# Gate and up tiles of a feed-forward layer as seven Strassen block products in place of eight

## The reference, cut to what matters

```python
def hybrid_layer(h, pos, states, p):
    u = rms_norm(h, p['norm_mix']) @ p['w_in']
    ...  # four groups of heads: SSD, retention, GLA, RG-LRU
    h = h + mixed.astype(h.dtype)          # mixed = concat(four outputs) @ w_out
    hn = rms_norm(h, p['norm_ffn'])
    h = h + ((jax.nn.silu(hn @ p['w_gate']) * (hn @ p['w_up'])) @ p['w_down']).astype(h.dtype)
```

## Time and profile before

| | us |
|---|---|
| median of 3 runs | 1392.7 |
| lowest, highest | 1392.46, 1395.43 |
| span of the profiled execution | 1392.0 |
| TensorE busy in it | 1361.7 |
| VectorE busy | 630.7 |
| ScalarE busy | 492.6 |
| GpSimd busy | 409.9 |

### The profile page before, as it was taken

One profiled execution on the slowest core, in us unless ns is written; L12 is line 12 of the kernel. 1 busy time (PEld: TensorE's weight loads), 2 busy tenths in 40 slices (PEclk: granted clock), 3 DMA queues, 4 the chain that ended last, 5 costly groups with the idle time before them and its releaser, 6 DMA issues.

```text
span 1392.0 us, 26025 instructions
## 1 busy us (share of the span) xinstructions
PE 1361.7 (98%) x11309; PEld 1313.6 (94%) x11309; DVE 630.7 (45%) x1250; ACT 492.6 (35%) x675; POOL 409.9 (29%) x204
## 2 busy tenths in 40 slices
PE   7999999999999999999999999999999999999996
PEld 7888898999999999999998888899999999999996
DVE  6844765553321343133757456646443123322434
ACT  6526454432221222122553364543322122222221
POOL 1101001434433443344400100023334433443341
PEclk9999999999999999999999999999999999999998
DMA  7746633222222223222466465422222222222231
GB/s 248 182 106 154 160 80 104 89 88 81 88 91 92 83 85 91 91 87 81 130 139 156 119 156 130 106 79 90 78 91 80 89 92 92 82 86 92 91 92 65
DMA packets 42066, 146.68 MB, mean 105 GB/s; under 512 B 5216, under 2 KB 6496, under 8 KB 41952
## 3 DMA queue, kind: packets, MB, share of 16 engines
q1 hardware_dynamic: 30672, 111.95, 25.1%
q0 software_dynamic: 6624, 24.12, 10.4%
q10 hardware_dynamic: 4656, 8.95, 2.1%
HBM read 137.34 MB, written 5.43 MB: 103 GB/s over the span
## 4 chain that ended last, share of the span: by engine, by line
PE 85%; DVE 7%; ACT 3%; DVEq 2%; issue 1%; ACTq 1%; DMA 0%
PE bank L1261 78%; DVE ct L755 1%; PE bank L1209 1%; DVE lru_x L755 1%; PE bank L1518 1%; ACT wl L419 0%; PE bank L1524 0%; PE bank L1225 0%; DVEq L754 0%; PE bank L1220 0%; ACT wh L420 0%; DVE h L1200 0%; PE bank L1443 0%; DVE gl_gla L1186 0%; PE bank L1547 0%
## 5 line engine op out<-in xcount | busy, mean ns | idle before, releaser
L1261 PE MATMUL bank<-xh,wh 128*128 128x272 f32 x2208 | 649.8, 294 | 7.9 <-DVE xl L710 7.6
L1261 PE MATMUL bank<-xh,wl 128*128 128x272 f32 x2208 | 642.9, 291 | 0.0
L1261 PE MATMUL bank<-xl,wh 128*128 128x272 f32 x2208 | 639.3, 290 | 0.0
L391 POOL TENSOR_TENSOR wl<-raw,wh 128x1024 fp32r<-128x1024 f32 x154 | 369.7, 2400 | 591.0 <-ACT wh L420 572.1
L1261 PEld LDWEIGHTS bank<-xh,wh 128*128 128x128 f32 x2208 | 420.0, 190 | 19.4 <-issue 17.5
L420 ACT ACTIVATE wh<-raw 128x1024 fp32r<-128x1024 f32 x199 | 210.2, 1056 | 611.3 <-PE bank L1261 611.3
L1261 PEld LDWEIGHTS bank<-xl,wh 128*128 128x128 f32 x2208 | 420.5, 190 | 1.0 <-issue 1.0
L1261 PEld LDWEIGHTS bank<-xh,wl 128*128 128x128 f32 x2208 | 419.3, 190 | 0.0
L1178 DVE TENSOR_TENSOR tz<-bank,rs_bcast 128x272 f32<-128x272 f32 x176 | 77.6, 442 | 293.3 <-PE bank L1261 289.3
L1158 DVE TENSOR_TENSOR h<-h,bank 128x272 f32<-128x272 f32 x128 | 55.4, 436 | 217.3 <-PE bank L1261 217.2
L397 POOL DMA_DIRECT2D wl<-weights x46 | 40.0, 870 | 365.2 <-ACT wl L419 365.2
(11 more groups left out here) (360 smaller groups left out, 1721.1 us busy)
## 6 DMA issues: line engine op xcount, KB each, us to landing
raw<-weights SPq DMA_DIRECT2D x202, 512.0 KB, 3.6
wl<-weights POOLq DMA_DIRECT2D x46, 512.0 KB, 6.9
h<-x SPq DMA_DIRECT2D x4, 544.0 KB, 6.0
y<-h SPq DMA_DIRECT2D x4, 544.0 KB, 2.7
rv<-rk ACTq DMA_DIRECT2D x8, 136.0 KB, 4.0
tz<-rq ACTq DMA_DIRECT2D x8, 136.0 KB, 5.4
S<-s_ssd ACTq DMA_DIRECT2D x2, 512.0 KB, 7.0
n_ssd<-Vx ACTq DMA_DIRECT2D x2, 512.0 KB, 2.8
```

What stands on the lines that cost most here:

```text
L391: nc.gpsimd.tensor_tensor(wl[:, s, :], raw[:, s, :], wh[:, s, :].bitcast(F32), ALU.subtract).then_inc(lo_done, 1)
L1261: ins = mm(bank_, wt[:, n % RING, w], xx[:, cols], start=(i == 0 and j == 0), stop=(i == len(ks) - 1 and j == 2))
```

## The change

The product of one pair is seen as blocks of 2 x 2: the 8 k-tiles are split in even (e) and odd (o) ones, the tokens in `first` and `second` half, and the two outputs are gate and up. Plain, that is eight block products of 4 k-tiles x 272 tokens x 3 passes. The Winograd form of Strassen's scheme takes seven:

- P1 and P2 are plain (gate even x first, gate odd x first), P3 and P4 have a sum on one side, P5 to P7 on both. Gate first = P1 + P2, and the others are sums of P1, P6, P7 and P3, P4 or P5. On the weight side P5, P7, P6 and P4 need sums of blocks of the gate and up units, on the side of the activations P5, P7, P3 and P6.
- **Weight sums.** VectorE makes them for every pair in `wsum`: `weight_sums` (1024 columns), `second_sum` and `last_sum` (512 each). The remainders of P6 and P5 are made by VectorE (`sum_low`), those of P4 and P7 by GpSimd, those of P1, P2 and P3 by accumulating transfers of 512 columns. ScalarE rounds all seven blocks, and negates three.
- **Sums of the activations.** Once per layer, while the output units run: `next_part`, `sums_hi` on ScalarE, `part_low`, `x_sums`, `x_sums_low` on VectorE.
- **Taking the results.** ScalarE copies P1 (`take_p1`), P1 + P6 (`take_u2`) and P1 + P6 + P7 (`take_u3`) out of a bank on which TensorE then goes on adding. VectorE adds and scales: `gate_first`, `gate_second`, `up_second`, `product`, `product_low`. P4 and P3 of a pair are computed during the next pair.
- **The ring.** `raw` has four slots. `wh` and `wl` are rings of eight half units of 512 columns (`RING`, `NEXT`): a product takes one, a plain unit two. ScalarE prepares the block that takes the place of a product as soon as that product is done (`hi_after`).
- **Output units.** Their remainders come by accumulating transfers now, as those of the input units.
- **Banks of the norm.** The statistics in front of the feed-forward part use `dense` banks (`norm_banks`). TensorE's order there is P1, P2, P6 and P5 of pair 0, most of it ahead of the last tile, then the spread of the factors, then P7.

```diff
+RING = 8
+WIDE = [2 if kind == "unit" else 1 for _, kind, _ in STEPS]
...
 def low_by(j):
...
+    return {"P1": FROM_HBM, "P2": FROM_HBM, "P3": FROM_HBM, "P4": ON_POOL, "P5": ON_VECTOR, "P6": ON_VECTOR,
+            "P7": ON_POOL}[kind]
...
 @block.sync
+                    sp.wait_ge(hi_done, step(layer, "P3" if u > gate_unit(p) else "P2", p) + 1)
+                    sp.wait_ge(sum_made.sem, sum_made.at(layer, 3 * p + 3))
...
 @block.scalar
+            def hi_block(j):
+                layer, kind, i = STEPS[j]
+                if kind in SUM_PLACE:
+                    act.wait_ge(sum_made.sem, sum_made.at(layer, 3 * i + SUM_MADE[kind]))
+                    whole = sum_cols(kind)
...
+                if LOW_BY[j] == FROM_HBM:
+                    a(wl[:, place(j)], whole, ACT.Copy, scale=-1.0).then_inc(negated, 1)
+                a(wh[:, place(j)], whole, ACT.Copy).then_inc(hi_done, 1)
...
+                for g, (p0, n) in enumerate(GROUPS):
+                    for p in range(p0, p0 + n):
+                        if p:
+                            take_p1(p)
+                        hi_after(step(layer, "P1", p))
+                        hi_after(step(layer, "P2", p))
+                        if p > p0:
+                            hi_after(step(layer, "P4", p - 1))
+                        take_u2(p)
+                        hi_after(step(layer, "P6", p))
+                        if p > p0:
+                            silu(p - 1)
+                            hi_after(step(layer, "P3", p - 1))
+                        hi_after(step(layer, "P5", p))
+                        take_u3(p)
+                        if p > p0:
+                            act_high(p - 1)
+                        hi_after(step(layer, "P7", p))
...
 @block.vector
+                def weight_sums(p):
...
+                    tt(wsum[:, 0:2 * BLOCK], raw_cols(n + 1), raw_cols(n, BLOCK), ALU.subtract).then_inc(sum_made.sem, 1)
...
+                def sum_low(kind, p):
+                    j = step(layer, kind, p)
+                    dve.wait_ge(hi_done, j + 1)
+                    tt(wl[:, place(j)], sum_cols(kind), wh[:, place(j)].bitcast(F32), ALU.subtract).then_inc(lo_vector, 1)
...
+                    for p in range(p0, p0 + n):
+                        more = p + 1 < p0 + n
+                        if more:
+                            weight_sums(p + 1)
+                        gate_first(p)
+                        if more:
+                            second_sum(p + 1)
+                        if more:
+                            last_sum(p + 1)
+                        if p > p0:
+                            gate_second(p - 1)
+                        if more:
+                            sum_low("P6", p + 1)
+                        if p > p0:
+                            product(p - 1)
+                        if more:
+                            sum_low("P5", p + 1)
+                        if p > p0:
+                            product_low(p - 1)
+                        up_second(p)
...
 @block.tensor
+                    for k in steps:
...
+                        for pass_, (wt, xx) in enumerate(((wh, hi), (wh, lo), (wl, hi))):
+                            ins = mm(b[:, 0:HALF], wt[:, at:at + P], xx,
...
+                product("P5", 0, rest, True)
+                spread_rstd(layer, 0)
+                product_7(0)
...
+                def product_7(p):
+                    pe.wait_ge(u2_taken.sem, u2_taken.at(layer, p + 1))
+                    product("P7", p)
...
+                        first_products(p)
+                        if p > p0:
+                            product_4(p - 1)
+                        product_6(p)
+                        if p > p0:
+                            product_3(p - 1)
+                        product_5(p)
+                        product_7(p)
```

More of the change, by code:

```diff
@@ L254, in trunk @@
         dense, M = bank[0:3], bank[3:8]
+        bank_a, bank_b, bank_c = M[0:2], M[2:4], M[4]
+        first, second = slice(0, HALF), slice(HALF, TOK)
         def cst(name, parts=P, lo=0, n=None):
@@ L1625, in _ @@
+                if layer:
+                    pe.wait_ge(c_taken.sem, c_taken.at(layer, 0))
+                product("P2", 0, some, True)
                 square_sums(layer, 0)
                 last_squares(layer, 0)
[L1627 to L1631 removed]
```

575 lines of the change are left out of this document (417 added, 158 removed).

## The result

| | before | changed |
|---|---|---|
| median, us | 1393.1 (1392.5 to 1395.4, four runs) | 1378.9 (1378.0 to 1382.2, four runs) |
| profiled execution, span | 1392.0 | 1376.9 |
| TensorE matmuls | 11309 | 10781 |

The ratio is 0.9895, with an interval from 0.9883 to 0.9908: faster by 1%, or 14 us, inside the range of 1341 to 1384. But the forecast was 1360, and less than half of the gain that it promised is there. The 528 matmuls are gone as counted; 66.4 us less TensorE work has become 15.1 us less span.

The account below looks back on a forecast made before the run. TensorE's matmul count was taken as the bound: 66.4 us saved, less 12 (group stalls), 17 (layer entries), 4 (other entries) and 1.6 (tails), leaves 31.8 off 1392.0, plus 0.7 to the median: 1360 us, range 1341 to 1384.

Parts of the forecast that it names:

- The entry's idle time: Before P7 of pair 0 in each layer: TensorE idles 6.0 us; with slow clock and table load 17 us for both.
- The entries of the four other groups: At the start of the groups that don't open a layer: P7 waits for roundings and bank copy, 1 us x 4.
- the rival of late loads: Up-weight loads landing in about 6.5 us make the loop 12.5 us, total 1381; chance 0.15.
- the one that ends slower: Loads landing in 7.2 us or more use up the gain, 1418 at 8.3 us; chance 0.07.
- The rival of the falling clock: TensorE's clock falls at each of 14 stalling pairs, 1.5 us each, 21 more, total 1381; chance 0.05.
- the lock: VectorE operations with two SBUF inputs stand still until GpSimd's subtraction ends: loop 11.5 us, 9.0 without it.
- the stall inside the groups, "12 us": In the pair loop of the six groups: 11.5 us a pair against TensorE's 10.57 stalls TensorE 12 us in all.
- e = 0.91: Excess of the loop per pair over TensorE's 10.57 us, with GpSimd's half operation taken at 1.25 us.
- 20e - 6: Total group stall: 4e - 1 in each of four groups of eight, 2e - 1 in each of two of six.
- The tail of a group of six: Last activation ready about 9.5 us after its P7, needed at 8.7: 0.8 us, twice, 1.6 in all.
- The stretch at the lower clock: Behind each layer entry's idle gap: some 15 matmuls slower by 0.10 us each, 1.5 us a layer.
- The loop fits: GpSimd's operations fall into VectorE's waits, loop under 10.57 us: 1349, or 1338 with a shorter entry; chance 0.20.

Follow-up runs that it names:

- experiment 11: Changed kernel with the output units' remainders made by GpSimd's subtractions again instead of accumulating transfers: 1378.0 us, ratio 0.988.
- Experiment 2: Changed kernel with VectorE's order alone changed, second_sum ahead of gate_first and gate_second ahead of last_sum: 1345.8 us, ratio 0.965.
- experiments 1: Changed kernel with GpSimd's remainders of P4 and P7 cut to 64 of 512 columns, the rest left out: 1352.0 us, ratio 0.969.
- 4: Changed kernel with the remainders of P4 and P7 on VectorE too, none of the sums' remainders on GpSimd: 1351.7 us, ratio 0.969.
- 5: Changed kernel with VectorE's second sum ahead of the gate, and at a layer's entry the bank copy and pair 1's first two sums earlier: 1337.9 us.
- 6: Kernel of 5, with ScalarE also rounding a group's last activation ahead of the roundings that follow P3: 1334.3 us, ratio 0.958.
- 7: Kernel of 6, with the remainders of P4 and P7 made by VectorE as well: 1328.9 us, ratio 0.954.
- 9: Kernel of 6, with all four remainders of the weight sums made by GpSimd: 1334.4 us, ratio 0.957.
- experiment 10: Changed kernel with only ScalarE's bank copy for P7 of pair 0 moved ahead of rounding pair 1's weights: 1377.1 us, ratio 0.987.

## Why the prediction was right in sign, with a gain twice too large

**Right.** 528 matmuls, at 0.126 us. The entry's idle time, 6.04 for 6.0, with its chain: L1369, three roundings, L799. The entries of the four other groups, forecast at 1 us each: 0.86 of wait, 1.02 of time, and 0.10 at the matmul behind. Output units at nothing (experiment 11). Loads: raw weights land in 4.3 us at the median (3.9 to 6.9) in the first group, estimated at 5.1 between 3.5 and 8.3; VectorE waits 6.2 us in total for them. One of the prediction's signs of being wrong, a sum of 1024 that waits for a DMA, is there in 5 of 44 sums, but the loads don't set the pace, so the rival of late loads, and the one that ends slower, fell. The rival of the falling clock fell: the short waits leave it at 1.00. And the lock: an operation with two SBUF inputs stands still until GpSimd's ends. The Trainium skill (SBUF — State Buffer, section on the two separate sides) calls the loser fully blocked; the trace agrees, 1.80 against 0.73 us, in all 44 pairs. The Trainium skill's rule for the two engines (the same page, section Summary: rules for kernel authors) ends: "Schedule whichever is off the critical path". Experiment 2 comes near to that and takes off 33 us. One working in the prediction is off, and nothing hangs on it: by its own steps the loop without the lock is 9.4 us, not 9.0.

**The step that failed: the stall inside the groups, "12 us".** It was 23; the mechanism was right and its size was not. How the 23 is measured comes first, then the two things that the 12 had wrong. The second of them is worked out from timelines, not from a run of its own.

- What the view of waits prints is not what a stall costs. [0.30 <-ACT u] stands between starts that are 0.59 apart instead of 0.126, so 0.46 is lost, and the matmul behind starts 0.23 later, 0.10 more. 0.56 for a printed 0.30. The 38 waits within the groups are 12.9 us as printed (28.4 less the entries' 15.5), and 12.9 + 38 x 0.26 = 22.8 us. The distances of the starts, added up one by one, give 23.0. This is also how 1.13 of excess a pair shows as two waits of 0.30 and 0.32.
- The excess per pair was taken as e = 0.91. It is 11.70 - 10.57 = 1.13. GpSimd's half operation, which no row showed, was taken at 1.25; it is 1.27 to 1.81, 1.29 at the median, and 1.37 at the first standstill of the pair shown. The rest of the excess is not assigned: 0.1 here and there in a chain of some fifteen events. By the prediction's formula, 20e - 6 = 16.6: 4.6 us of the error.
- The formula gives the groups 1 us of slack before the stall begins ("4e - 1", "2e - 1"), 6 us in all. It wasn't there: 20 x 1.13 is 22.6. In a second or third group, VectorE arrives at the sum for the third pair before its load does. VectorE in the changed kernel, second group of layer 0:

```profile
451.94 0.44 DVE L1458 TENSOR_TENSOR up<-bank,u 128x272 f32<-128x272 f32 x1 [1.12 <-ACT u L804]
453.67 1.23 DVE L1364 TENSOR_TENSOR wsum<-raw 128x1024 f32<-128x1024 f32 x1 [1.28 <-DMA raw<-weights]
464.67 0.44 DVE L1458 TENSOR_TENSOR up<-bank,u 128x272 f32<-128x272 f32 x1
```

  That pair takes 12.73 us. The load rival was priced as a setter of the pace in every pair; it comes once a group, in four of six, at 1.13 to 1.28 us, and that is enough to take the slack. In the layer's first group the slow clock and the silu's table load (1.28 at 319.69) may do the same. In layer 0 the first stall stands at the third pair's P7 in the first group and at the fourth's in the two others.

**Terms that were too small.** The tail of a group of six was "0.8"; it is 2.4 (printed as 0.55 and 1.49), and 0.2 in a group of eight: 5.5 us for 1.6. The step behind it took GpSimd's 2.4 us on the down weights into account but not that VectorE's last product stands still beside them as well. VectorE, then ScalarE and TensorE, in the changed kernel:

```profile
649.86 1.55 DVE L1463 TENSOR_TENSOR tz<-tz,rs_bcast 128x544 f32<-128x544 f32 x1 [0.83 <-ACT tz L808]
651.85 2.79 DVE L1467 TENSOR_TENSOR up<-up,tz 128x544 f32<-128x544 f32 x1
...
654.68 0.66 ACT L812 ACTIVATE gh_gla<-up 128x544 fp32r<-128x544 f32 x1 [3.08 <-DVE up L1467]
...
656.14 0.40 PE L1585 MATMUL bank<-gh_gla,wh 128*128 128x272 f32 x1 [1.49 <-DVE gl_gla L1473]
```

The multiply stands still for 0.8 and the product for 2.1. The stretch at the lower clock was sized from the earlier trace rows as 15 matmuls a layer; it was 24 in layer 0 and 25 in layer 1, of which 14 stand ahead of the stop: 19 more, 1.9 us. And the median lies 2.0 above this profiled execution's span, not 0.7: 1.3 us. Together: 11 for the stalls, 3.9 for the tails and 1.9 for the clock are 16.8; the silu's table load, which had 0.9 a layer of its own, is within the stalls, so 15.0 of the 16.7 us that the span has over the forecast one (1376.9 against 1360.2). Of the other 1.7 the 0.10 us at the matmul behind each of the four entries' and eight tails' stops are 1.2; I could put 0.5 to no line. The run median's 1.3 makes it 18.

**The rivals.** "The loop fits", at 1349 or with a shorter entry 1338, is where experiments 1, 2, 4 and 5 lie, and 6, 7 and 9 below it. It was given 0.20, on the ground that GpSimd's operations might fall into VectorE's waits. They don't in this order, but they needn't: it is enough that they hit something that nobody waits for. With the order of experiment 2 the change would have been worth 49 us, and 64 with all three edits of order and no sharing. So the 66.4 us of the matmuls could be had almost whole, and what was missing was lost by the order of the other engines' work.

**Open.** Why the wait of 1.69 on L793 is gone when VectorE makes all remainders is not known; that it is gone was read from two traces. The load that is late once a group was not taken away by itself. How much of experiment 2's 33 us is the place of the standstills, and how much their move to GpSimd or the shorter chain, was not separated.

## What to carry over

When two engines lock each other out, don't count the standstill, place it: write down the loop as a chain of who waits for whom, and give the engine that must stand still something that nobody waits for at that point. Sharing the remainders with GpSimd cost 27 us in one order (1378.9 against 1351.7 with all on VectorE) and 5 in the other (1334.3 against 1328.9), and in the bad order twice the GpSimd work was 14 us faster. Work that is added beside a bound engine is only free as long as its chain, and not its busy share (64% here), is shorter than the bound engine's step; and a slack of 1 us in such a chain is to be checked against each load and table load that can eat it once.

## What the hardware showed that I had not expected

- The standstill goes both ways: GpSimd's subtraction of 512 columns takes 1.29 us at the median in the changed kernel, and 1.78 in experiment 2 at 350.98, where VectorE's product came first.
- The same stop of TensorE of 6.04 us had 24 matmuls at the lower clock level behind it in layer 0 and 11 in layer 1. A wait of 1.49 us had none behind it. In experiment 10 a wait of 2.37 us had none either in layer 0, but one of 1.77 us that came 5 us later had 14.
- A printed wait of 0.3 us at TensorE costs 0.56 in the distances between the starts of its matmuls.
